# Gate products of the recurrent branch in two row halves of the array, and the fifth and sixth chunk's steps moved to later rounds

## The chip, the cores and the metric

The kernel runs on one core of a Trainium2 chip. The metric is the device time of the whole program in microseconds (us). A core has five engines that run side by side, each through its own instruction list in order: TensorE (PE, matrix products into PSUM), VectorE (DVE), ScalarE (ACT), GpSimd (POOL) and SyncE (SP), which here only issues DMA transfers. They wait for one another through semaphores.

## The reference, cut to what matters

One layer of a streaming encoder runs on 2048 prompt tokens and 64 sample tokens. The change touches one of its two token mixers, the recurrent one (RG-LRU), with 512 channels in eight blocks of 64:

```
xb = x.reshape(B, T, 8, 64)
r  = sigmoid(einsum('btni,nij->btnj', xb, wa) + ba)      # gate a
ig = sigmoid(einsum('btni,nij->btnj', xb, wx) + bx)      # gate x
log_a = -8 * r * softplus(-lam);  a = exp(log_a)
u  = sqrt(-expm1(2 * log_a)) * (ig * x)
h_t = a_t * h_{t-1} + u_t                                 # a scan over the tokens
rnn = h * gelu(rg)
```

`x` is here a causal convolution of width 4 of one projection (`rx`), `rg` is another. The gates are therefore block-diagonal products: channel block n reads only its own 64 channels. The other mixer is attention over a band of 512 past tokens. Both are projected from the same normed input by one wide matrix, `w_in`.

## The kernel before, in words

The program has stages one behind the other: modulation and values (to about 145 us), the projections (145 to 769 us), attention (from 769 us), the merge of the two mixers, the output projection, and the feed-forward part.

The stage in question is the projection stage. It has 16 rounds, four for each j = 0..3; a j is 128 of the 512 recurrent channels. Round i = r % 4 of a j is of kind RECUR (i = 0: `rx` and `rg`), GATES (i = 1 and 3: merge gates) or HEADS (i = 2: queries and keys). A round is seven products c = 0..6 of a fast matrix scheme (sums and differences of quarter matrices, as in Strassen's). Each product has three column pieces q of 352 tokens, and each piece 12 matmuls (four contraction tiles by three passes over f16 high and low parts): 36 matmuls for a product, 252 for a round, all in `passes` at L2988. PE also makes the gate products, six chunks s = 0..5 of 353 tokens for each j (L3029, `gate_products`): six matmuls each, two gates by three passes, into PSUM banks 4 and 5. `GATE_SLOTS` says behind which product of which round they stand.

The other engines run the lists that are written out for each round:

- ACT splits the next weights into their high part (`proj_hi`, L1377), copies products out of PSUM (`copy`, L1398, and `c21`, L1416 to L1419), applies the gate functions (`gates`: L1482 and L1485 read banks 4 and 5 with tanh, L1488 and L1489 make tanh and exp), takes the root (`root`, L1494, which needs another function table than tanh), and makes high parts: of a chunk (`chunk_hi`), of the recurrent output (`rnn_hi`, L1500), of the queries (`q_hi`, L1441) and of the keys (`k_hi`, L1447).
- DVE makes the low parts of all these (`proj_lo` L2159, `rnn_lo` L2307, `q_lo` L2231, `k_lo` L2236), adds products up (`p_block`, L2220 to L2226), makes the convolution (`conv`), and the recurrence (`recur1`, `recur2` with the scan at L2282 or L2287, `rnn_product` L2301).
- SP issues, in this order, in the loop over rounds: the next round's weights, then in i = 1 and i = 2 the stores of the recurrent output, then in i = 3 the stores of queries and keys. Behind the last round it issues the loads of the attention stage.

```
                if i == 2:
                    for s in range(3, NS):
                        recurrent_store(j, s)      # waits x_lo: the low part of chunk s
                if i == 3:
                    head_row(j, 0)                 # waits qk_lo: queries' low part
                    new_keys(j)                    # waits qk_hi: keys' high part
                    head_row(j, 1)                 # waits qk_lo: keys' low part
```

PE may not write product c = 2 before ACT has copied c = 0 of the same piece out of its bank, nor c = 4, 5, 6 before the copies of c = 2, 3, 4; a gate product waits for its chunk's low part (`x_xlo`); and product c = 1 of rounds 1 to 3 waits, as `gates_before` says, until ACT has read the gate products out of bank 4.

## Time and profile before

| | |
|---|---|
| median of three runs | 2694.84 us (2688.36 to 2695.31) |
| span of the profiled execution | 2692.3 us, 2.5 us under that median |
| PE busy | 2645.6 us, 98% of the span |
| DVE, ACT, POOL busy | 65%, 51%, 23% |
| mean granted clock of PE | 0.992 of full speed |
| chain that ended last | PE 84%, DVE 5%, ACT 4%, DMA 3%, issue 2% |

The profiled execution's own time is its span, from the first to the last instruction, and the little that lies around it; the medians of runs take in both. An engine's busy share is a mean over all stages, so what a change in one stage is worth is read in that stage.

### The profile page before, as it was taken

Reading aid. Unit: us, or ns where it says so; the run is one execution under the profiler, and the core shown is the slowest. Engines: PE = TensorE matmul, PEld = TensorE weight load, DVE = VectorE, ACT = ScalarE, POOL = GpSimd, SP = SyncE. Lnnn points to the kernel's source line nnn. Section 1 sums busy time; section 2 is a strip of 40 time slices with the busy share of each in tenths; the row PEclk is TensorE's granted clock in tenths of the full one; section 3 lists DMA queues with packets and bytes.
Section 4 is the critical chain, followed back from the end, with each engine's and each line's share of the span. In section 5 each row is a group of like instructions: output and inputs, shape, how many; then the busy total and the mean of one; then the engine's idle time right before and its main releaser. Section 6 shows DMA issues by size and latency. Waiting matters only on the chain.

```text
span 2692.3 us, 50625 instructions
## 1 busy us (share of the span) xinstructions
PE 2645.6 (98%) x18664; PEld 1771.5 (66%) x18664; DVE 1750.8 (65%) x3367; ACT 1362.9 (51%) x2666; POOL 628.2 (23%) x698
## 2 busy tenths in 40 slices
PE   7999999999999999999999999999999999999998
PEld 2466666666668888557996666666666666666665
DVE  4966464655646666776778788888888875242433
ACT  4967474755656666113556555565555653121211
POOL 2600000000008889000000254433344311101000
PEclk9999999999999999999999999999999999999999
DMA  8621322031294442556552354445545438567572
GB/s 281 200 74 66 135 78 105 25 109 71 93 231 95 112 156 105 183 210 202 143 142 69 126 181 166 171 168 189 181 159 179 165 120 325 212 233 262 210 249 106
DMA packets 238419, 423.07 MB, mean 157 GB/s; under 512 B 57816, under 2 KB 162776, under 8 KB 230056
## 3 DMA queue, kind: packets, MB, share of 16 engines
q1 hardware_dynamic: 229400, 412.03, 46.1%
q10 hardware_dynamic: 8848, 8.74, 1.0%
q8 instruction: 109, 1.79, 0.3%
q14 instruction: 62, 0.51, 0.1%
HBM read 283.42 MB, written 139.92 MB: 157 GB/s over the span
## 4 chain that ended last, share of the span: by engine, by line
PE 84%; DVE 5%; ACT 4%; DMA 3%; issue 2%; POOL 1%; SPq 0%; DVEq 0%; ACTq 0%; POOLq 0%
PE ps L2988 57%; PE ps L3240 14%; PE ps L3080 4%; PE ps L3067 3%; PE ps L3056 2%; DMA arena<-in_w_mod_rest 2%; PE ps L2912 1%; ACT arena L1600 1%; PE ps L3094 1%; POOL arena L1140 1%; PE ps L3029 1%; DVE arena L2393 1%; DVE arena L2471 1%; ACT arena L1607 1%; DVE arena L2089 0%
## 5 line engine op out<-in xcount | busy, mean ns | idle before, releaser
L2988 PE MATMUL ps<-arena 128*128 128x352 f16 (+1 forms) x11880 | 1613.1, 297 | 5.1 <-ACT arena L1768 2.1
L2988 PEld LDWEIGHTS ps<-arena 128*128 128x128 f16 x11880 | 1100.6, 97 | 513.1 <-ACT arena L1768 2.5
L3240 PE MATMUL ps<-arena 128*128 128x352 f16 x2772 | 414.9, 310 | 0.5 <-DVE arena L2689 0.5
L3240 PEld LDWEIGHTS ps<-arena 128*128 128x128 f16 x2772 | 264.7, 96 | 150.8 <-issue 1.0
L1197 POOL TENSOR_TENSOR arena<-arena 128x128 f32<-128x128 f32 x44 | 30.6, 695 | 740.4 <-DMA arena<-in_w_down 740.1
L3094 PE MATMUL ps<-arena 128*128 128x424 f16 (+1 forms) x960 | 172.5, 341 | 2.1 <-DVE arena L2471 1.4
L1760 ACT ACTIVATE arena<-ps 128x352 f32<-128x352 f32 x264 | 116.3, 460 | 98.8 <-PE ps L2988 98.8
L1153 POOL CAST arena<-arena 64x512 f16<-64x512 f32 x8 | 4.9, 610 | 689.6 <-DMA arena<-in_cache_kT 689.3
L3080 PE MATMUL ps<-arena 128*128 128x64 f32 (+2 forms) x1200 | 151.0, 272 | 0.5 <-DVE arena L2435 0.5
L1207 POOL TENSOR_TENSOR arena<-arena 128x176 f32<-128x176 f32 (+1 forms) x57 | 56.2, 986 | 398.4 <-DMA arena<-ffn_hidden 398.4
L3080 PEld LDWEIGHTS ps<-arena 128*128 128x128 f32 (+2 forms) x1200 | 144.4, 193 | 3.4 <-issue 2.1
L3094 PEld LDWEIGHTS ps<-arena 128*128 128x128 f16 x960 | 92.1, 96 | 82.0 <-DVE arena L2471 2.2
L1398 ACT ACTIVATE arena<-ps 128x352 f32<-128x352 f32 x192 | 81.0, 463 | 123.2 <-PE ps L2988 123.2
L2792 DVE TENSOR_TENSOR arena<-ps,arena 128x352 f32<-128x352 f32 x12 | 6.3, 525 | 206.3 <-PE ps L3240 176.4
L2592 DVE SCALAR_TENSOR_TENSOR arena<-arena 128x512 f16<-128x512 f32 x154 | 105.4, 715 | 49.4 <-ACT arena L1722 49.4
L1607 ACT ACTIVATE arena<-ps 128x512 f32<-128x512 f32 (+3 forms) x136 | 76.3, 561 | 104.7 <-PE ps L3067 104.6
L2660 DVE SCALAR_TENSOR_TENSOR arena<-arena 128x2114 f32<-128x2114 f32 x44 | 110.1, 2502 | 27.1 <-ACT arena L1797 27.0
L1181 POOL TENSOR_TENSOR arena<-arena 128x1024 f32<-128x1024 f32 (+6 forms) x147 | 119.7, 814 | 13.6 <-POOL arena L1174 3.7
L2159 DVE SCALAR_TENSOR_TENSOR arena<-arena 128x512 f16<-128x512 f32 x112 | 73.9, 687 | 64.1 <-ACT arena L1377 63.9
L1953 ACT ACTIVATE arena<-ps 128x352 f32<-128x352 f32 x12 | 5.6, 464 | 205.7 <-PE ps L3240 205.7
L2664 DVE SCALAR_TENSOR_TENSOR arena<-arena 128x2114 f32<-128x2114 f32 x44 | 108.8, 2473 | 0.3
L1797 ACT ACTIVATE arena<-arena 128x2114 f32<-128x2114 f32 x44 | 94.5, 2147 | 26.7 <-DVE arena L2647 26.4
(239 smaller groups left out, 3587.1 us busy)
## 6 DMA issues: line engine op xcount, KB each, us to landing
hidden_combinations<-arena SPq DMA_DIRECT2D x48, 616.0 KB, 3.2
arena<-hidden_combinations SPq DMA_DIRECT2D x24, 1232.0 KB, 7.8
arena<-in_w_up SPq DMA_DIRECT2D x44, 512.0 KB, 4.9
down_combinations<-arena SPq DMA_DIRECT2D x44, 448.0 KB, 2.8
ffn_hidden<-arena SPq DMA_DIRECT2D x44, 440.0 KB, 3.1
arena<-down_combinations SPq DMA_DIRECT2D x10, 1792.0 KB, 7.8
arena<-down_combinations SPq DMA_DIRECT2D x20, 896.0 KB, 6.9
arena<-ffn_hidden SPq DMA_DIRECT2D x50, 352.0 KB, 3.9
```

The source lines that it names most:

```text
L1181: pool.tensor_tensor(out, djunk[:, :, 0:w], djunk[:, :, w:2 * w], ALU.add).then_inc(ada_step, 1)
L1398: act.activation(pcp[(0, 1, 2, 0)[i]][q], ps[:, bank, 0:CF], ACT.Copy, scale=CSF).then_inc(p_cp, 1)
L1607: act.activation(pt[:, x.h, 0:m * P], ps[:, 4, 0:m * P], ACT.Copy).then_inc(t_act, 1)
L1760: act.activation(fcp[(0, 1, 2, 0)[i]][q], ps[:, bank_of((0, 2, 3, 4)[i], q), 0:CF], ACT.Copy, scale=CSF)\
L1797: act.activation(out, u[:, 0:LF], ACT.Identity, scale=w0, bias=fb).then_inc(f_tap, 1)
L2592: dve.scalar_tensor_tensor(fsp[:, c, :, 1, :], src.rearrange("p (k m) -> p k m", k=4), -WSF if c == 6 else WSF, fsp[:, c, :, 0, :], ALU.mu ...
L2660: dve.scalar_tensor_tensor(out, u[:, 1:1 + LF], tap(1), out, ALU.mult, ALU.add).then_inc(f_conv, 1)
L2664: dve.scalar_tensor_tensor(out, u[:, 2:2 + LF], tap(2), out, ALU.mult, ALU.add).then_inc(f_conv, 1)
L2988: mm = pe.matmul(out, wt[:, k, wp, :], act_t[:, k, hp], start=(first and k == 0 and n == 0), stop=(last and k == K - 1 and n == 2), skip_g ...
L3080: mm = pe.matmul(ps[0:x.rows, 6, 64 * x.h:64 * x.h + 64], pt[0:k, x.h, c * P:c * P + x.rows], vv[x.b][0:k, x.v0 + c, 64 * x.h:64 * x.h + 6 ...
L3094: mm = pe.matmul(out, wt[:, wp, k, :], mixT[:, k, hp, t:t + w], start=(k == k0 and m == 0), stop=(k == k1 - 1 and m == 2))
L3240: mm = pe.matmul(ps[:, down_bank(n, k), 0:CF].rearrange("p (w t) -> p w t", w=2), dwt(i)[:, wi, wp, :], dact[i][:, :, bi, hp, :], start=(i ...
```

## The change

Two things are done at once.

1. The gate weights were a matrix of 128 by 128 for each gate, zero outside its two blocks. Now the two gates share one matrix of 128 by 128: gate a has its blocks on the diagonal, gate x off it (the input that holds gate x's bias is shifted by 64 rows to match). A gate product is six matmuls again, but each takes only 64 rows of the array: channels 0 to 63 with all 128 weight columns go to bank 4, channels 64 to 127 to bank 5, in turn. Bank 4 then holds gate a for the low channels and gate x for the low channels in its upper half; bank 5 the same for the high channels. ACT reads each half by itself: four tanh of 64 partitions in place of two of 128.
2. The steps of the fifth and sixth chunk (s = 4 and 5), and the root of the fourth, move to later rounds on PE, ACT and DVE. SP's list stays as it was.

```
-            return NS * j + (0, 2, 5, 6)[i]
+            return NS * j + (0, 2, 4, 6)[i]          # gates_before
...
             def gates(j, s):
-                act.wait_ge(x_gate, 2 * n + 1)
+                low, high = slice(0, 64), slice(64, 128)
+                act.wait_ge(x_gate, 2 * n + 2)
                 act.wait_ge(x_conv, 3 * n + 3)
-                act.activation(cols, ps[:, 4, 0:w], ACT.Tanh, scale=0.5 * CS, bias=half_bias(0, j)).then_inc(x_act, 1)
-                act.wait_ge(x_gate, 2 * n + 2)
+                act.activation(cols[low], ps[low, 4, 0:w], ACT.Tanh, scale=0.5 * CS, bias=half_bias(0, j)[low])
+                act.activation(cols[high], ps[high, 5, 0:w], ACT.Tanh, scale=0.5 * CS, bias=half_bias(0, j)[high])\
+                    .then_inc(x_act, 1)
-                act.activation(bufI[s % 2][:, 0:w], ps[:, 5, 0:w], ACT.Tanh, scale=0.5 * CS, bias=half_bias(1, j)).then_inc(x_act, 1)
+                act.activation(bufI[s % 2][low, 0:w], ps[high, 4, 0:w], ACT.Tanh, scale=0.5 * CS,
+                               bias=half_bias(1, j)[high])
+                act.activation(bufI[s % 2][high, 0:w], ps[low, 5, 0:w], ACT.Tanh, scale=0.5 * CS,
+                               bias=half_bias(1, j)[low]).then_inc(x_act, 1)
...
             def gate_products(j, s):
-                r = 4 * j + (0, 0, 1, 1, 1, 2)[s]
+                r = 4 * j + (0, 0, 1, 1, 2, 2)[s]
-                for g in range(2):
-                    for m, (wp, hp) in enumerate(PASSES):
-                        mm = pe.matmul(ps[:, 4 + g, 0:w], gws[:, wp, P * g:P * g + P], xsp[hp][:, 0:w],
+                for m, (wp, hp) in enumerate(PASSES):
+                    for g in range(2):
+                        own = slice(64 * g, 64 * g + 64)
+                        mm = pe.matmul(ps[:, 4 + g, 0:w], gws[own, wp, :], xsp[hp][own, 0:w],
                                        start=(m == 0), stop=(m == 2))
-                    mm.then_inc(x_gate, 1)
+                        if m == 2:
+                            mm.then_inc(x_gate, 1)
...
-            GATE_SLOTS = {(0, 3): 0, (0, 5): 1, (1, 2): 2, (1, 4): 3, (1, 6): 4, (2, 2): 5}
+            GATE_SLOTS = {(0, 3): 0, (0, 5): 1, (1, 2): 2, (1, 4): 3, (2, 2): 4, (2, 4): 5}
```

The rest of the diff moves the calls. On ACT the root of chunk 3 goes from the end of round 1 to the start of round 2, `gates(4)`, `root(4)`, `rnn_hi(4)` and `gates(5)` spread over round 2, and `root(5)`, `q_hi`, `rnn_hi(5)` go into round 3. The largest shift is at the head of the fourth round of each j. On DVE, these are the rows of the end of round 2 and the start of round 3 for the last j, before (L2278 to L2301 is the recurrence of chunk 5, L2307 `rnn_lo`, L2231 `q_lo`, L2236 `k_lo`, L2220 `p_block` of product c = 1):

```order
L2278 TENSOR_TENSOR arena<-arena 128x350
L2287 SCALAR_TENSOR_TENSOR arena<-arena 128x283
L2288 SCALAR_TENSOR_TENSOR arena<-arena 128x64
...
L2307 SCALAR_TENSOR_TENSOR arena<-arena 128x350
L2159 SCALAR_TENSOR_TENSOR arena<-arena 128x4x128
L2223 SCALAR_TENSOR_TENSOR arena<-ps,arena 128x352 x2
L2223 SCALAR_TENSOR_TENSOR arena<-ps,arena 128x320
L2223 SCALAR_TENSOR_TENSOR arena<-ps,arena 128x32
L2231 SCALAR_TENSOR_TENSOR arena<-arena 128x2115
L2159 SCALAR_TENSOR_TENSOR arena<-arena 128x4x128 x2
L2236 TENSOR_TENSOR arena<-arena 128x2115
L2220 SCALAR_TENSOR_TENSOR arena<-ps,arena 128x352 x2
```

The same place on DVE in the changed kernel, whose lines stand five higher (L2283 to L2306 the recurrence, L2236 `q_lo`, L2225 `p_block`, L2241 `k_lo`, L2312 `rnn_lo`):

```order
L2164 SCALAR_TENSOR_TENSOR arena<-arena 128x4x128 x2
L2283 TENSOR_TENSOR arena<-arena 128x350
L2292 SCALAR_TENSOR_TENSOR arena<-arena 128x283
L2293 SCALAR_TENSOR_TENSOR arena<-arena 128x64
...
L2306 TENSOR_TENSOR arena<-arena 128x64
L2236 SCALAR_TENSOR_TENSOR arena<-arena 128x2115
L2225 SCALAR_TENSOR_TENSOR arena<-ps,arena 128x352 x2
L2225 SCALAR_TENSOR_TENSOR arena<-ps,arena 128x320
L2225 SCALAR_TENSOR_TENSOR arena<-ps,arena 128x32
L2241 TENSOR_TENSOR arena<-arena 128x2115
L2312 SCALAR_TENSOR_TENSOR arena<-arena 128x350
```

The recurrence of chunk 5 and `q_lo` have moved behind the two `proj_lo` that open round 3, `k_lo` behind the sums of product c = 1, and `rnn_lo(5)` from the middle of round 2 to behind `k_lo`.

On ACT the head of round 3 for the last j read so before (L1416 to L1419 `c21`, L1377 `proj_hi`, L1447 `k_hi`, L1398 the copies; `q_hi`, L1441, stands at the end of round 2):

```order
L1441 ACTIVATE arena<-arena 128x2115
L1416 ACTIVATE arena<-ps 128x352 x2
L1418 ACTIVATE arena<-ps 128x320
L1419 ACTIVATE arena<-ps 128x32
L1377 ACTIVATE arena<-arena 128x4x128 x2
L1447 ACTIVATE arena<-arena 128x2115
L1398 ACTIVATE arena<-ps 128x352 x12
```

And so in the changed kernel (L1499 `root`, L1505 `rnn_hi`):

```order
L1377 ACTIVATE arena<-arena 128x4x128 x2
L1499 ACT_TABLE_LOAD
L1499 ACTIVATE arena<-arena 128x350
L1441 ACTIVATE arena<-arena 128x2115
L1398 ACTIVATE arena<-ps 128x352 x3
L1447 ACTIVATE arena<-arena 128x2115
L1505 ACTIVATE arena<-arena 128x350
L1398 ACTIVATE arena<-ps 128x352 x9
```

The table load, the root and `q_hi` now stand ahead of the copies of c = 0, and `k_hi` and `rnn_hi(5)` behind them.

SP's list for the same place is word for word that of before (L734 to L737 stores of the recurrent output, L722 and L723 of queries and of keys, L775 and L778 the first loads of the attention stage); the waits of each row stand in brackets:

```order
L734 DMA recurrent_outputs<-arena 256x1x353 [waits x_lo] x2
L736 DMA recurrent_outputs<-arena 256x1x283 [waits x_lo]
L737 DMA recurrent_outputs<-arena 256x1x64
L722 DMA queries<-arena 256x1x2048 [waits qk_lo]
L723 DMA queries<-arena 256x1x64
L727 DMA out_k_prompt<-arena 128x512 [waits qk_hi]
...
L722 DMA keys<-arena 256x1x2048 [waits qk_lo]
L723 DMA keys<-arena 256x1x64
L775 DMA arena<-queries 64x2112 [waits k_stored,q_stored,p_filled]
```

What has moved is only when `x_lo` of chunk 5 and the two `qk_lo` come, on which these rows wait.

## Rows read from the trace of the kernel before

**Rows 1.** The page: busy time by engine.

```profile
PE 2645.6 (98%) x18664; PEld 1771.5 (66%) x18664; DVE 1750.8 (65%) x3367; ACT 1362.9 (51%) x2666; POOL 628.2 (23%) x698
```

**Rows 2.** Stretches: the second and fourth round of j = 1, and round 15.

```profile
340.80:381.10 40.30, 40.30 (x272) 26.07 (x271) 28.39 (x56) 32.03 (x53) 0.00 (x0) 1.00 0.12 41
419.50:457.20 37.70, 37.70 (x255) 24.40 (x253) 14.29 (x24) 15.53 (x27) 0.00 (x0) 1.00 0.27 94
731.00:768.50 37.50, 37.50 (x254) 24.22 (x251) 8.88 (x17) 12.94 (x22) 0.00 (x0) 1.00 0.89 232
```

The columns are the stretch, its length, busy us (and instructions) of PE, PEld, DVE, ACT and POOL, the granted clock, the DMA share and GB/s.

**Rows 3.** Timeline of PE around a gate product: start, us, instruction.

```profile
167.09 1.06 PE L3029 MATMUL ps<-arena 128*128 128x353 f16 x6
167.99 10.90 PE L2988 MATMUL ps<-arena 128*128 128x352 f16 x72
```

**Rows 4.** Timeline of PE: full-height, then half-height matmuls between those of L2957.

```profile
115.61 1.02 PE L2957 MATMUL ps<-arena 128*128 128x512 f16 x4
116.47 0.60 PE L2927 MATMUL ps<-arena 128*128 128x128 f32 x4
...
126.74 0.81 PE L2957 MATMUL ps<-arena 128*128 128x512 f16 x3
127.48 0.43 PE L2927 MATMUL ps<-arena 64*128 64x64 f32 x2
127.84 0.39 PE L2957 MATMUL ps<-arena 128*128 128x512 f16 x1
...
840.33 0.40 PE L3067 MATMUL ps<-arena 64*128 64x64 f32 x4
```

**Rows 5.** Groups of ACT in round 2 of j = 1.

```profile
L1398 ACT ACTIVATE arena<-ps 128x352 f32<-128x352 f32 x12 | 4.9, 467 | 1.9 <-PE ps L2988 1.9
L1494 ACT ACT_TABLE_LOAD x2 | 2.6, 1283 | 0.0
L1482 ACT ACTIVATE arena<-ps,arena 128x350 f32<-128x350 f32 x1 | 0.6, 554 | 0.0
```

**Rows 6.** Timelines of ACT and DVE: round 2 of j = 1, then round 15.

```profile
406.99 0.81 DVE L2287 TENSOR_TENSOR_SCAN arena<-arena 128x283 f32<-128x283 f32 x1
410.91 0.52 DVE L2307 SCALAR_TENSOR_TENSOR arena<-arena 128x350 f16<-128x350 f32 x1
...
731.63 1.15 ACT L1377 ACTIVATE arena<-arena 128x512 f16<-128x512 f32 x2
732.67 1.97 ACT L1447 ACTIVATE arena<-arena 128x2115 f16<-128x2115 f32 x1
734.67 2.36 DVE L2236 TENSOR_TENSOR arena<-arena 128x2115 f16<-128x2115 f32 x1 [1.08 <-ACT arena L1447]
741.96 0.59 DVE L2220 SCALAR_TENSOR_TENSOR arena<-ps,arena 128x320 f32<-128x320 f32 x2 [1.26 <-PE ps L2988]
```

**Rows 7.** Timeline of SP's queue in round 15.

```profile
730.86 0.51 SPq L722 DMA_DIRECT2D queries<-arena  x1
735.05 1.63 SPq L728 DMA_DIRECT2D out_k_sample<-arena  x1
741.95 1.16 SPq L775 DMA_DIRECT2D arena<-queries  x2
763.03 0.59 SPq L787 DMA_DIRECT2D arena<-in_cache_v  x1
```

**Rows 8.** DMA busy tenths, 731 to 769 us, in 40 slices.

```profile
DMA  0999351499501999999999999999998999999996
```

**Rows 9.** Landing of L787, and PE where attention begins.

```profile
DMA to landing us min/median/max: 4.7/5.0/5.4
...
772.07 0.34 PE L3080 MATMUL ps<-arena 128*128 128x64 f32 x2
```

**Rows 10.** Stretches around a pause of PE.

```profile
1500.00:1508.00 8.00, 5.89 (x41) 3.61 (x39) 5.01 (x11) 4.12 (x8) 1.88 (x4) 1.00 0.31 100
1508.00:1511.40 3.40, 3.40 (x13) 1.70 (x12) 3.40 (x4) 3.40 (x5) 2.09 (x2) 0.50 0.20 73
```

72 lines of the change are left out of this document (36 added, 36 removed).

## The prediction

> **What bounds the kernel now.** I read the page first: PE is busy 98% of the span [rows 1], so where PE never waits, only less PE time or a new wait of PE can move the end. Then the stretches: in the second and the fourth round of j = 1 and in round 15, PE is busy for exactly the length of the stretch, at full granted clock, while ACT has 32.03 of 40.30 us in round 1 and 15.53 of 37.70 us in round 3 [rows 2]. The reader is to see that this stage is PE alone: ACT and DVE are only of interest where they come so late that PE would stop, and the work moved from round 1 to rounds 2 and 3 moves from a full list to an empty one without gaining anything by itself. Last I read the place where the stage hands over to attention: there the DMA engines are at 9 tenths or more in nearly all slices from 743 us on [rows 8]. Nothing waits for them yet, but with little to spare, as worked out below.
>
> **Term 1, the gate products.** The six matmuls of L3029 start at 167.09 us and the next L2988 at 167.99 us: 0.90 us, or 0.15 us for each [rows 3]. There are 24 such groups, 21.6 us in all. The changed group has as many matmuls of as many columns, but in three pairs whose two members use different rows of the array and different banks. If the members run side by side, three pairs take 3 x 0.15 = 0.45 us; if not, 0.90 us as before. No row shows two half-height matmuls in different halves, so both stay in the range. I take side by side, because two matmuls on separate rows share neither weights nor outputs, and give the other a chance of its own below. The Trainium skill says the same ("TensorE: Matmul & The Clock Gate", measured speedup vs the span model: tiles of one packing start about 4 ns apart). By that rule a pair would be an estimated 0.154 us, and the group 0.46 us; no run here shows it yet.
>
> What speaks against it is the border between full and half height. Four L2957 matmuls before a full-height L2927 start at 115.61 us, 0.215 us apart by their width and clock, and L2927 starts at 116.47 us, just 4 x 0.215 us later: no delay. Before the half-height L2927, three start at 126.74 us, so the last at 127.17 us, and L2927 starts at 127.48 us: 0.31 us behind it, 0.09 us more than its streaming. A matmul's time has a tail behind its streaming: a single L2957 takes 0.39 us, 0.18 us over its 0.215 us. Four half-height ones in a row take 0.40 us, less that tail 0.07 us apiece. The two of L2927 should then need 0.14 us until the next can start, but that starts at 127.84 us, 0.36 us behind the first: 0.22 us more. Half of it, 0.11 us, lies between the two (0.43 us in all, less 0.25 us for the second, less 0.07 us), and is theirs as f32 with a weight load of their own, as I read it; the other half is the way out [rows 4]. I take the way in and the way out, 0.09 + 0.11 = 0.20 us a group, and keep 0 and the whole 0.31 us as bounds. The changed group is then 0.45 + 0.20 = 0.65 us, which saves 0.25 us, times 24 = **6.0 us**. Bounds: 0.14 x 24 = 3.4 us and 0.45 x 24 = 10.8 us. The Trainium skill has a rule for this border ("TensorEngine Tiling (Array Packing)", key properties: a change of tiling mode drains TensorE, a change of tile does not); the 0.09 us ahead of the half-height L2927 agrees with it [rows 4]. By its reading every group pays twice, as the sum has it.
>
> **Term 2, ACT and DVE within the rounds: nothing.** Four tanh of 64 partitions replace two of 128. A tanh on 353 columns takes 0.55 us [rows 5]; columns set its length, so two more cost 1.1 us a chunk, two chunks in a round, 2.2 us. If halves took half the time it would be nothing. Round 1 has 8 us of ACT free [rows 2], loses `root(3)` with the table loads that it brought (1.28 us each [rows 5]) and the fifth chunk. Where could PE stop? Time is counted from a round's start, and a product is 36 x 0.149 = 5.4 us, so c = 2 starts at 10.7 us and needs the first copy of c = 0 by then.
> - Round 2: ACT's first part is as before until about 3.2 us, then root(3) (1.28 + 0.5), `rnn_hi(3)` behind the scan and the product on DVE (2.3 us) and its own 0.5 us: 7.8 us. The first copy takes 0.47 us [rows 5], ready at 8.3 us: 2.4 us to spare. Later, gates(4) with its table load ends near 21.5 us and root(4) near 24.6 us; the copies of c = 3 are done by 25.8 us and wanted from 27.4 us on: 1.6 us or more to spare.
> - Round 3: `proj_hi` starts 0.6 us into the round and takes 1.05 us [rows 6], root(5) ends at 3.5 us, DVE's recurrence of chunk 5 at 5.4 us (its scan is 0.81 us [rows 6]), `q_hi` as long as `k_hi`, 1.97 us, at 7.4 us. First copy at 7.9 us: 2.8 us to spare.
> If the cover of 1.6 us were gone, each us beyond would cost 4 us, once for every j. What is late next is only what waits for the low parts: the queue.
>
> **Term 3, the handover to attention: 5.5 us lost.** SP's list is in order. The stores of queries and keys, and behind them the first loads of attention, stand behind the store of chunk 5, which waits for `rnn_lo(5)`. That used to be done in round 2: at 410.91 us for j = 1 [rows 6], 8.6 us before round 3. Now it stands behind `k_lo` in round 3. For the last j, counted from 731.0 us:
> - `q_hi` 7.4, `q_lo` as long as `k_lo`, 2.36 us: 9.8. `p_block` of c = 1 can't end before PE has made it: as now, 741.96 + 0.59 us [rows 6], so 11.5. `k_hi` behind three copies: 8.5 + 1.97 = 10.5, no wait. `k_lo` 11.5 + 2.36 = 13.9. `rnn_lo(5)` 0.52: 14.4.
> - SP: two stores of chunk 5 in 1.2 us (each issue as the 0.51 us of L722, and the rest between), queries 1.2, new keys 2.0 (L728 alone 1.63), keys 1.2 [rows 7]: 20.0 us. The load of L775 is issued there. Now it is issued at 741.95 us, 10.95 us in [rows 7]. It is 9.05 us late.
> - By the DMA engines' time it is more. Now the stores of queries and keys lie in two bursts in the first 12 slices, whose tenths add up to 64, so 6.1 us and, since a 9 is 90% or more, up to 6.9 us: 6.5 us. The loads fill every slice from the 14th on, 12.4 us in, and the first burst begins 1.1 us behind its issue [rows 7, 8]. Then the stores' transfer begins at 15.6 + 1.1 = 16.7 us in one piece, ends at 23.2 us, and the loads' behind it: 10.8 us late.
> The last of the values (L787) is issued at 763.03 us and lands 4.7 us later, 767.7 us [rows 7, 9]. PE wants it for the first L3080 at 772.07 us [rows 9]: 4.4 us to spare. So PE stops for 9.05 - 4.4 = 4.7 us by SP's time, or 10.8 - 4.4 = 6.4 us by the DMA engines'. I take the middle, 5.5 us. PE's own end moves with round 15, so nothing of term 1 gives cover here. For j = 0 to 2 the same lateness hits the weights for the next round 0, due by the end of round 3, 20 us later: nothing.
>
> **Term 4, the clock.** At 1500 us PE is busy 5.89 of 8.00 us, and the next 3.40 us run at a granted clock of 0.50, the 1.2 GHz level, with PE busy throughout [rows 10]: half of that, 1.7 us, was lost. A stop of some 5 us at the handover should bring such a stretch. Attention's first units leave PE partly idle anyhow, so I take 1.0 us, between 0 and 1.7 us.
>
> **Sum.** -6.0 + 0 + 5.5 + 1.0 = +0.5 us. On the profiled span of 2692.3 us that is 2692.8 us; on the median, 2.5 us higher, **2695.3 us**. Its own range: -8.6 (borders cost 0.09 us) + 4.7 + 0 = -3.9 us, to -3.4 + 6.4 + 1.7 = +4.7 us: 2691 to 2700 us.
>
> **The rivals.**
> - *The handover costs nothing.* DVE, ACT or the stores are faster than I chained them, or the loads don't need the time they take now, so that the 4.4 us hold. For it: a slice or two ahead of the loads are empty today [rows 8], and the stores might move beside the loads. Against it: a lateness of 9 us is twice the reserve. It gives -6.0 us, 2688.8 us; with free borders -10.8 us, 2684 us. Only below a group of 0.56 us does this end faster than can be told. Chance 0.20.
> - *The halves don't run side by side* (the change doesn't do what it says, slower). Then a group is 0.90 + 0.20 us: +4.8 us in place of -6.0 us, and with the handover 4.8 + 6.5 = +11.3 us, 2706.1 us. It decides from a pair of 0.26 us on, where 24 x 3 pairs x 0.11 us have made the time 8.1 us longer than my sum. For it: no row shows two halves at once. Against it: they share nothing. Chance 0.15.
> - *Copies come late in rounds 2 or 3.* ACT now waits there for a scan on DVE ahead of the copies of c = 0. If the chain is 2 us longer than its spare, PE stops 2 us in each j: 0.5 + 8 = +8.5 us, 2703.3 us. Against it: 1.6 to 2.8 us to spare by durations that overlap by 0.1 us each. Chance 0.05.
>
> **How the numbers follow.** Mine 0.60, the rivals 0.20, 0.15, 0.05. About 0.3%, 8.1 us, is what a measurement of this kernel can tell from no change: below 2686.8 us it is faster, above 2702.9 us slower. Faster: 0.07 of the free handover, 0.03 of mine, 0.10. Slower: 0.13 of the halves, 0.03 of the copies, 0.01 of mine, 0.17. The same: 0.73. The range 2687 to 2706 us leaves out some 0.10 below and 0.09 above.
>
> **What would show it.** The start of L2988 behind a gate group, minus the group's start: 0.65 us if right, 1.1 us if the halves take turns. PE's idle time in 145 to 763 us: none. SP's first L775: 20 us behind the start of round 15. PE's idle time at the first L3056, L3067 and L3080, put down to DMA, band, values or queries: 5 to 7.5 us, and a granted clock of 0.50 behind it. The prediction is wrong if PE doesn't wait there, or if the group isn't between 0.45 and 0.76 us.

## The result and the profile after

| | before | changed |
|---|---|---|
| median of five runs each | 2695.14 us | 2738.13 us (2730.72 to 2740.86) |
| span of the profiled execution | 2692.3 us | 2736.3 us |
| ratio, 95% interval | | 1.0156 (1.0141 to 1.0171): slower by 42 us |

The prediction was 2695.3 us, 2687 to 2706 us. The time lies 32 us above the top of the range.

The page of the changed kernel, busy time by engine (against [rows 1]):

```profile
PE 2649.0 (97%) x18664; PEld 1763.3 (64%) x18664; DVE 1751.6 (64%) x3367; ACT 1393.0 (51%) x2714; POOL 628.9 (23%) x698
```

PE has 3.4 us more busy time, and the span is 44 us longer: PE waits more. So the first question is where. I cut both spans at PE's own instructions: the projection stage runs from the first start to the last start of a product matmul of 352 columns, the handover from there to the first start of L3080 (L3087 in the changed kernel).

| us | before | changed | difference |
|---|---|---|---|
| ahead of the projection stage | 145.6 | 144.8 | -0.8 |
| projection stage | 622.9 | 659.7 | +36.9 |
| handover to attention | 3.6 | 11.1 | +7.5 |
| attention, merge and the rest | 1920.2 | 1920.7 | +0.5 |

**The part that was right.** Timeline of PE around a gate product (the place of [rows 3]):

```profile
166.37 0.62 PE L3035 MATMUL ps<-arena 64*128 64x353 f16 x6
166.92 10.91 PE L2993 MATMUL ps<-arena 128*128 128x352 f16 x72
```

The next product starts 0.55 us behind the group's start; before it was 0.90 us. The rest of the cost stands ahead of the group: its first matmul starts 0.245 us behind the last full-height one, where two full-height ones are 0.149 us apart. The whole group then costs 0.651 us, for which the prediction had 0.65 us. In single records the two members of a pair start 4 ns apart.

**Where PE stops.** Waits of PE in the changed kernel (what it waited for, us in total, times, longest). Before, PE had no wait in the projection stage at all:

```profile
PE ps L3035 <- DVE arena L2225: 26.6, 4, 7.4
PE ps L2993 <- ACT arena L1416: 5.6, 5, 1.2
PE ps L3063 <- DMA arena<-keys: 5.1, 1, 5.1
PE ps L2993 <- ACT arena L1419: 1.0, 4, 0.2
PE ps L3087 <- DMA arena<-in_cache_v: 1.4, 1, 1.4
```

The first row is the answer: once for every j, PE waits 6.4 to 7.4 us at one gate group. It is the group of chunk 4, which the change moved behind product c = 2 of round 2. Timeline of PE in round 2 of j = 1 (the round starts at 388.97 us):

```profile
388.97 3.74 PE L2993 MATMUL ps<-arena 128*128 128x352 f16 x24 [1.24 <-ACT arena L1416]
392.95 12.81 PE L2993 MATMUL ps<-arena 128*128 128x352 f16 x84 [0.24 <-ACT arena L1419]
412.12 1.07 PE L3035 MATMUL ps<-arena 64*128 64x353 f16 x6 [6.36 <-DVE arena L2225]
413.12 13.37 PE L2993 MATMUL ps<-arena 128*128 128x352 f16 x72
```

The 72 matmuls behind the stop take 13.37 us, where 72 others took 10.91 us. The stretches show why (length, busy of PE, PEld, DVE, ACT, POOL, granted clock, DMA share, GB/s):

```profile
406.80:412.10 5.30, 0.00 (x0) 0.01 (x1) 1.69 (x7) 0.00 (x0) 0.00 (x0) 0.60 1.01 412
412.10:418.10 6.00, 5.98 (x24) 2.82 (x25) 4.74 (x9) 4.23 (x7) 0.00 (x0) 0.50 0.09 24
```

While PE stands, the granted clock falls to 0.50, the 1.2 GHz level, and here it stays there for the first 6 us of full work; at the other three places for 2.8 to 3.3 us. At the four places together, the matmuls behind the groups take 5.2 us more than at full clock, and four small waits of 0.11 us at product c = 2 make it 5.7 us.

**What the stop waits for.** The gate products go to banks 4 and 5, where product c = 1 of the same round stands until DVE has read it. So PE waits for the sums L2225 of product c = 1, and DVE had long been idle. DVE in the same round:

```profile
396.84 0.53 DVE L2283 TENSOR_TENSOR arena<-arena 128x353 f32<-128x353 f32 x1 [6.44 <-ACT arena L1499]
397.40 0.95 DVE L2287 TENSOR_TENSOR_SCAN arena<-arena 128x353 f32<-128x353 f32 x1
398.68 0.53 DVE L2306 TENSOR_TENSOR arena<-arena 128x353 f32<-128x353 f32 x1
399.77 0.53 DVE L2312 SCALAR_TENSOR_TENSOR arena<-arena 128x353 f16<-128x353 f32 x1 [0.57 <-ACT arena L1505]
400.22 1.29 DVE L2164 SCALAR_TENSOR_TENSOR arena<-arena 128x512 f16<-128x512 f32 x2
410.41 1.45 DVE L2225 SCALAR_TENSOR_TENSOR arena<-ps,arena 128x352 f32<-128x352 f32 x4 [8.91 <-DMA gates<-arena]
```

DVE waits 8.91 us for a store: L2225 writes into the row buffer from which SP still stores the gate row of round 1. SP's queue, changed kernel:

```profile
401.53 0.81 SPq L690 DMA_DIRECT2D arena<-in_w_proj  x2
402.38 0.43 SPq L716 DMA_DIRECT2D gates<-arena  x1
403.89 0.99 SPq L717 DMA_DIRECT2D gates<-arena  x1
```

And before:

```profile
384.40 0.80 SPq L690 DMA_DIRECT2D arena<-in_w_proj  x2
385.25 0.43 SPq L716 DMA_DIRECT2D gates<-arena  x1
```

SP's list is in order. The store of the gate row (L716, L717) stands behind the load of the next weights (L690), which waits until DVE has made the low parts of this round's last two weight tiles (L2164). Before, these were made 3.4 us into the round. Now they stand behind `recur2`, the product and `rnn_lo` of chunk 3, and these behind the moved root(3) (L1499): L2164 ends 12.5 us into the round, and L690 is issued at once. The whole chain, read backwards: PE's gate group, DVE's sums, the stores, SP's weight load, DVE's low parts, DVE's recurrence of chunk 3, ACT's root(3). Each link is one row above. The wait itself is not new: before, the group of chunk 5 stood behind c = 2 of round 2 and waited for the same sums. That round starts at 381.04 us:

```profile
393.19 1.45 DVE L2220 SCALAR_TENSOR_TENSOR arena<-ps,arena 128x352 f32<-128x352 f32 x4
397.15 1.05 PE L3029 MATMUL ps<-arena 128*128 128x350 f16 x6
```

There the sums began 12.2 us into the round, now 21.4 us, and the group, 16.1 us in, did not stop. So what costs the time is the late store, and not that another chunk's group now stands in that place.

Adding up PE's start-to-start times over the whole stage gives its parts, in us over what 4031 matmuls of 352 columns take at 0.1487 us each:

| | before | changed |
|---|---|---|
| 24 gate groups | 21.6 | 44.3 = 24 x 0.65 + 28.7 |
| half clock behind them, with the four small waits | 0 | 5.7 |
| stops at copies (L1416, L1419) | 0 | 8.0 |
| all small rest | 1.9 | 2.3 |

The 28.7 us are what the four groups of chunk 4 take (7.5 to 8.5 us each) beyond 0.65 us. The differences, 22.7 + 5.7 + 8.0 + 0.4, are the stage's +36.9 us.

**The handover.** SP, PE and DVE in the changed kernel around the last round, which starts at 767.05 us (against [rows 7, 9]):

```profile
778.50 2.35 DVE L2241 TENSOR_TENSOR arena<-arena 128x2115 f16<-128x2115 f32 x1
780.77 0.52 DVE L2312 SCALAR_TENSOR_TENSOR arena<-arena 128x350 f16<-128x350 f32 x1
...
787.65 2.15 SPq L775 DMA_DIRECT2D arena<-queries  x2
...
809.88 0.59 PE L3063 MATMUL ps<-arena 128*128 128x128 f16 x4 [5.06 <-DMA arena<-keys]
812.01 0.60 PE L3063 MATMUL ps<-arena 128*128 128x256 f16 x2 [1.55 <-DVE arena L2419]
815.64 0.69 PE L3087 MATMUL ps<-arena 128*128 128x64 f32 x2 [1.40 <-DMA arena<-in_cache_v]
```

`k_lo` (L2241) ends 13.8 us and `rnn_lo(5)` (L2312) 14.2 us into the round; the prediction had 13.9 and 14.4. L775 is issued 20.6 us into it; the prediction had 20.0. So the chain of term 3 on DVE and SP happened nearly as written. On PE's side it did not quite: the prediction let PE stop for the values (L787) at the first L3080, but the largest part, 5.06 us, was a wait for the keys at the first L3063, and 1.40 us one for the values.

### The profile page after: what moved, and what is told of

The parts are those of the page before. It is cut to its first block, busy times and chain, and to the rows that moved or that the text cites. A ratio compares the mean times of both kernels' runs of the same rounds, so it can differ in the third digit from the quotient of the medians.

```text
span 2736.3 us, 50651 instructions
## 1 busy us (share of the span) xinstructions
PE 2649.0 (97%) x18664; PEld 1763.3 (64%) x18664; DVE 1751.6 (64%) x3367; ACT 1393.0 (51%) x2714; POOL 628.9 (23%) x698
## 4 chain that ended last, share of the span: by engine, by line
PE 77%; ACT 7%; DVE 6%; DMA 3%; issue 3%; POOL 1%; SPq 1%; DVEq 0%; ACTq 0%; POOLq 0%
PE ps L2993 47%; PE ps L3247 15%; PE ps L3101 5%; PE ps L3087 4%; PE ps L3074 3%; PE ps L3063 2%; DMA gates<-arena 1%; PE ps L2917 1%; ACT arena L1605 1%; DMA arena<-in_w_down 1%; POOL arena L1140 1%; DVE arena L2253 1%; ACT arena L1315 1%; ACT arena L1281 1%; ACT arena L1612 1%
## 5 line engine op out<-in xcount | busy, mean ns | idle before, releaser
L2993 PE MATMUL ps<-arena 128*128 128x352 f16 (+1 forms) x11880 | 1619.2, 298 | 12.6 <-ACT arena L1416 5.6
L2993 PEld LDWEIGHTS ps<-arena 128*128 128x128 f16 x11880 | 1099.4, 97 | 531.2 <-issue 11.1
L3087 PE MATMUL ps<-arena 128*128 128x64 f32 (+2 forms) x1200 | 151.0, 271 | 1.9 <-DMA arena<-in_cache_v 1.4
L3087 PEld LDWEIGHTS ps<-arena 128*128 128x128 f32 (+2 forms) x1200 | 144.6, 192 | 4.6 <-DMA arena<-in_cache_v 1.7
L2597 DVE SCALAR_TENSOR_TENSOR arena<-arena 128x512 f16<-128x512 f32 x154 | 105.0, 713 | 46.1 <-ACT arena L1727 46.1
L1398 ACT ACTIVATE arena<-ps 128x352 f32<-128x352 f32 x192 | 79.4, 458 | 93.1 <-PE ps L2993 93.1
L1808 ACT ACTIVATE arena<-arena 128x1057 f32<-128x1057 f32 x44 | 45.3, 1076 | 124.9 <-DVE arena L2669 124.9
L1605 ACT ACTIVATE arena<-arena 128x640 f32<-128x640 f32 (+5 forms) x136 | 102.8, 756 | 10.0 <-DVE arena L2419 9.8
```

The costliest lines, as they stand in the source:

```text
L1605: act.activation(pr[0:x.rows, x.h, 0:x.w], pr[0:x.rows, x.h, 0:x.w], ACT.Exp, scale=-1.0, bias=least[0:x.rows, x.h:x.h + 1], accum_out=sm[ ...
L2597: dve.scalar_tensor_tensor(fsp[:, c, :, 1, :], src.rearrange("p (k m) -> p k m", k=4), -WSF if c == 6 else WSF, fsp[:, c, :, 0, :], ALU.mu ...
L2993: mm = pe.matmul(out, wt[:, k, wp, :], act_t[:, k, hp], start=(first and k == 0 and n == 0), stop=(last and k == K - 1 and n == 2), skip_g ...
L3087: mm = pe.matmul(ps[0:x.rows, 6, 64 * x.h:64 * x.h + 64], pt[0:k, x.h, c * P:c * P + x.rows], vv[x.b][0:k, x.v0 + c, 64 * x.h:64 * x.h + 6 ...
```

## The experiments

Fourteen kernels. All ratios are against the kernel before, in runs on the same chip; stage and handover are cut as in the table above. Before has 622.87 and 3.61 us, the changed kernel 659.72 and 11.14 us.

| run | stage | handover | median (before beside it) | ratio, 95% interval |
|---|---|---|---|---|
| e1 gate stores first | 625.75 | 10.95 | 2705.00 (2694.24) | 1.0040 (1.0027 to 1.0054) |
| e2 halves only | 630.13 | 3.61 | 2701.90 (2694.24) | 1.0027 (1.0012 to 1.0043) |
| e3 moves only | 652.75 | 10.44 | 2729.13 (2694.24) | 1.0137 (1.0102 to 1.0172) |
| e4 split low parts first | 626.25 | 10.89 | 2704.50 (2694.24) | 1.0042 (1.0026 to 1.0057) |
| e5 head rows first | 625.76 | 5.56 | 2699.59 (2694.01) | 1.0016 (1.0005 to 1.0028) |
| e6 first copy first | 623.80 | 6.22 | 2697.71 (2694.01) | 1.0014 (1.0003 to 1.0025) |
| e7 halves in turn | 625.90 | 10.61 | 2705.02 (2694.01) | 1.0037 (1.0024 to 1.0050) |
| e8 moves, stores first | 622.88 | 10.59 | 2700.86 (2694.01) | 1.0027 (1.0017 to 1.0037) |
| e9 whole copy first | 622.18 | 5.98 | 2696.02 (2695.21) | 1.0008 (0.9997 to 1.0019) |
| e10 loads first | 622.19 | 3.72 | 2697.67 (2695.21) | 1.0012 (1.0000 to 1.0024) |
| e11 all in time | 618.08 | 3.61 | 2693.15 (2692.98) | 0.9998 (0.9986 to 1.0010) |
| e12 as e11, full height | 622.88 | 3.61 | 2700.31 (2692.98) | 1.0020 (1.0008 to 1.0032) |
| e13 last rows first | 618.09 | 3.61 | 2691.47 (2692.80) | 0.9988 (0.9977 to 1.0000) |
| e14 as e13, full height | 622.88 | 3.61 | 2697.57 (2692.80) | 1.0011 (1.0000 to 1.0023) |

**e1, the stores ahead of the weights.** The theory is the chain above; the rival is that the low parts or the recurrence themselves are too late for PE. Only SP's list changes:

```
                 j, i = r // 4, r % 4
+                if i == 2:
+                    gate_row(r - 1, 0)
+                    gate_row(r - 1, 1)
                 if r + 1 < NR:
                     round_tiles(r + 1)
...
-                if r and kind_of(r - 1) == GATES:
+                if r and i == 0:
                     gate_row(r - 1, 0)
```

> The changed kernel, but in round 2 of each j SP issues the stores of the merge gates' rows ahead of the next round's weights, not behind them. Theory (queue): the 6.4 to 7.4 us for which PE stops at the fifth chunk's gate products are the landing of these stores, on which DVE's sums of product c = 1 wait; they are late only because the weights ahead of them wait for the low parts of products 5 and 6, now behind the fourth chunk's recurrence. Then the wait of 26.6 us and most of the half-clock stretch behind it go: 2738 - 27 - 7 = 2704 us, between 2700 and 2709 us. Rival (load): DVE and ACT are late by themselves in round 2 and the store only ends last by a little; then another releaser takes its place, and no more than a third goes: above 2725 us. Rival (half height): the products in halves cost the time; then nothing changes, 2738 us.

Measured: 2705.0 us. SP in the same round, and what is left of the waits in the stage:

```profile
382.86 0.33 SPq L716 DMA_DIRECT2D gates<-arena  x1
385.73 0.46 SPq L717 DMA_DIRECT2D gates<-arena  x1
391.88 0.81 SPq L690 DMA_DIRECT2D arena<-in_w_proj  x2
...
PE ps L2996 <- ACT arena L1419: 5.6, 5, 1.2
PE ps L2996 <- ACT arena L1422: 1.0, 4, 0.2
```

The weights are as late in the round as in the changed kernel (12.6 us into it, since this one starts at 379.3 us), and PE doesn't mind. The wait at the gate group is gone in all four j, the stage is 34.0 us shorter. One line's place in SP's list was 31 us of the 42 us by the ratios.

**e4, the other link of the chain.** In place of SP's order, DVE makes the low parts ahead of the recurrence of chunk 3:

```
+                if i == 2:                    # behind proj_lo of products 5 and 6
+                    recur2(j, 3)
+                    rnn_product(j, 3)
+                    rnn_lo(j, 3)
...
-                if i == 1:                    # ahead of them
-                    recur2(j, 3)
-                    rnn_product(j, 3)
-                    rnn_lo(j, 3)
```

> The changed kernel, but on DVE the low parts of products 5 and 6 stand ahead of the fourth chunk's recurrence at the start of round 2. SP's list is not touched. Theory (queue): the weights and behind them the gate rows' stores are issued some 6 us earlier (about 3 to 4 us into the round, as before the change), land near 12 us, and PE's 6.4 us stop shrinks to under 1 us: 2700 to 2710 us. Rival (load): the recurrence itself makes DVE late, and it is still there: above 2725 us. If only e1 helps, it is the weights' transfer ahead of the stores and not the recurrence.

Measured: 2704.5 us, stage 626.25 us. Cutting the chain at either link gives the same, within 0.5 us of the stage: it is one chain.

**e2 and e3, each half of the change alone.** e2 keeps every step at its place of before and has the products in halves. e3 has the moved steps and the full-height products. In both, `gate_products` names the round of chunk 4 to match its slot.

```
e2: with the changed gates() and gate_products(), but
             GATE_SLOTS = {(0, 3): 0, (0, 5): 1, (1, 2): 2, (1, 4): 3, (1, 6): 4, (2, 2): 5}
e3: with the gates() and gate_products() of before, but
             GATE_SLOTS = {(0, 3): 0, (0, 5): 1, (1, 2): 2, (1, 4): 3, (2, 2): 4, (2, 4): 5}
```

> The kernel before with the gate products in two row halves and the four half tanh, but every step of chunks 4 and 5 where it was. Theory (queue): the group costs 0.65 us in place of 0.90 us, so -6 us, and ACT in round 1 gets three chunks of two more tanh (3.3 us) against about 2 us that its copy of the next round's first product has to spare, so PE stops 1 to 4 us in each j: -6 + (4 to 16) = 2693 to 2705 us. The handover to attention stays as before. Rival (half height): the products themselves cost the time, and this kernel is near 2738 us.

> The kernel before with the moved steps of the fourth to sixth chunk alone; the gate products have full height and ACT reads them with two tanh. Theory (queue): all of the loss is in the moves: PE stops in round 2 of each j for the stores as in the changed kernel, and at the handover to attention, so 2738 + 6 us for the full-height groups, less up to 6 us since ACT ends round 1 earlier: 2738 to 2744 us. Rival (half height): near 2695 us. Rival (load, ACT): without the longer tanh ACT is in time, and the wait is much shorter: 2710 us or less.

Measured: e3 2729.13 us, e2 2701.90 us. The moved steps alone bring the stop, of 4.9 us at most and 19.5 us in all, so shorter than with halves (26.6 us); e3 is 9 us faster than the least that I had expected. But the halves alone are slower than before as well, by 7.3 us of stage, although each group costs 0.65 us. ACT and PE in e2, end of round 1 of j = 1:

```profile
379.23 0.50 ACT L1475 ACTIVATE arena<-arena 128x353 f16<-128x353 f32 x1
...
380.39 0.63 PE L3035 MATMUL ps<-arena 64*128 64x353 f16 x6 [1.41 <-issue]
381.65 17.95 PE L2993 MATMUL ps<-arena 128*128 128x352 f16 x108 [0.63 <-ACT arena L1416]
```

The group of chunk 4, with the wait at the copy behind it, costs 2.8 us there, in every j. It needs `chunk_hi(4)` (L1475) and DVE's low part (0.53 us) behind it, and L1475 ends at 379.73 us: as I read it, the two more tanh of each of its chunks (0.55 us apiece) made it late, since the full-height kernel of before has no stop there. Added up as above, e2's groups take 10.2 us beyond 24 x 0.65 us (four of 2.8 us, and three of chunk 5 of 1.2 us), the half clock behind them 1.6 us, one copy 0.8 us and the rest 0.6 us more: 13.2 - 5.9 = 7.3 us. So with halves ACT's list of round 1 is too long as it stands. Whether another order in it would have done as well as moving work out, no run tells: none has halves, nothing moved and another order. My view of [rows 2], 8 us of ACT free in round 1, did not show that: the free time lies elsewhere in the round than at its end.

**e8, the moves with the stores first.** The edit of e1 on e3:

> e3 (moves alone, full-height products) with the gate rows' stores ahead of the weights in round 2. Theory (queue): e3's 19.5 us of waits and the half clock behind them go, and the 7 us of the handover stay: 2695 + 7 = 2702 us, 2699 to 2705 us. Against e1 it tells what the halves are worth by themselves: -6 us of the groups and about +7 us of the late copy, so no difference. Rival (load): the recurrence moved into rounds 2 and 3 makes DVE late itself: above 2712 us.

Measured: stage 622.88 us, before's to 0.01 us, and handover 10.59 us, 7.0 us above before's. The run is 7.3 us slower (ratio 1.0027; 6.9 us by the medians). With the stores in place the moved steps cost nothing in the stage, and all that they lose is the handover. Between e8 and e1 the stage with halves is 2.9 us longer, though the groups save 5.9 us: the stops at copies (the rows under e1) take 8.0 us and smaller waits 0.8 us, and e8 has none of them. So these stops belong to the halves and not to the moved steps.

**e7, the halves one behind the other.** e1 with the loops exchanged, so that a half's three passes stand together:

```
-                for m, (wp, hp) in enumerate(PASSES):
-                    for g in range(2):
+                for g in range(2):
+                    for m, (wp, hp) in enumerate(PASSES):
```

> e1, but the three passes of one half stand ahead of the three of the other, so that only the third of the one and the first of the other can lie side by side. Theory (side by side): a group then takes 5 times 0.15 us and the borders' 0.20 us, 0.95 us in place of 0.65 us, times 24 = 7 us more than e1: 2712 us. Rival (the saving is only that half-height matmuls are cheap): as e1, 2705 us.

Measured: 2705.02 us, and my expectation was wrong. Timeline of PE:

```profile
165.53 0.63 PE L3038 MATMUL ps<-arena 64*128 64x353 f16 x6
166.10 10.91 PE L2996 MATMUL ps<-arena 128*128 128x352 f16 x72
```

The group takes 0.57 us from its start to the next product, as in pairs. Six in turn would take 0.90 us. The list has three matmuls of rows 0 to 63 and then three of rows 64 to 127; in the single records the starts are still in pairs, 10 ns apart instead of 4. So this run says nothing on what pairs are worth (e12 and e14 do), but, if the instructions reach PE in the order of the kernel's text, that PE ran a matmul of the one half past two of the other. The trace records neither that order nor which half a matmul is on, so this is my reading of the starts. The Trainium skill says the contrary of the reading ("TensorE: Matmul & The Clock Gate", part 3 on packing small matmuls: matmuls start and end strictly in program order). The group's length here does not agree. That the rival (half-height matmuls that are merely cheap, one behind the other) is wrong, the same starts tell: two lie 4 or 10 ns apart, and the next two follow 0.15 to 0.16 us later.

**e5, the order of the last stores.** e1, and SP stores chunk 5 behind the queries, the new keys and the keys:

```
                 if i == 2:
-                    for s in range(3, NS):
+                    for s in range(3, NS - 1):
                         recurrent_store(j, s)
                 if i == 3:
                     head_row(j, 0)
                     new_keys(j)
                     head_row(j, 1)
+                    recurrent_store(j, NS - 1)
```

> e1 and in SP's list the sixth chunk's store behind the stores of queries and keys, not ahead of them. Theory (queue): at the handover to attention PE stops from its last product to the first L3080 for 10.95 us in e1 against 3.61 us before, since the loads of keys, bias and values start some 9 us late behind that store. Ahead of it they start about 4 us late, and the stores before them are spread: 4 to 5.5 us to the first L3080, so 5 to 7 us less, with the half-clock stretch there shorter by some: 2697 to 2700 us. Rival (the loads are slow for another reason, as the DMA engines being full): no more than 2 us less.

Measured: handover 5.56 us against 10.95 us, 2699.59 us. So the store of chunk 5 ahead of the heads' stores is shown to be the cause of 5.4 of the 7.3 us that e1's handover has over that of before; most of the rest goes with e10.

**e6 and e9, copies ahead of high parts.** e6 is e5 with ACT's first two copies of round 1's last product ahead of `chunk_hi(4)`, and with DVE's low part of chunk 4 behind the sums of c = 5 of round 1. e9 is e6 with the third copy there too, taken from the start of round 2:

```
e6: -                if i == 1:
    -                    chunk_hi(j, 4)
                     if i == 1:
                         c21(r, 0)
                         c21(r, 1)
    +                    chunk_hi(j, 4)
    ...
    +                for q in range(3):
    +                    p_block(r, 1, q)
                     if i == 1:
                         chunk_lo(j, 4)
    -                for q in range(3):
    -                    p_block(r, 1, q)
e9: +                    c21(r, 2)
```

> e5 and, at the end of round 1, ACT copies the first two pieces of the last product ahead of the fifth chunk's high part, and DVE makes that chunk's low part behind its sums of c = 5. Theory (queue): PE stops 1.2 and 0.2 us in each j for that copy because it stands behind a chunk whose convolution comes late; these 6.6 us and the tails with them go, and what is left of the change is the groups' 6 us: about 7 us under e5, 2689 to 2693 us, at or under the kernel before. Rival (load): ACT's list of round 1 is too long with the tanh in halves, and the copy stays late: under 2 us less than e5.

> e6 with the third piece's copy too ahead of the merge gates' tanh at the end of round 1. In e6 PE still stops 1.3 us in each j, for this piece: it stands behind a tanh that waits for DVE's sums of c = 5. Theory (queue order): these four stops go, with the small ones behind them, 5 to 6 us less than e6 in the projection stage, which then takes 618 us: 2691 to 2694 us. Rival (the list of ACT is too long in round 1 with halves): the stop moves to a later copy in round 2 and the stage stays above 622 us, 2697 us.

Measured: stages of 623.80 and 622.18 us, medians of 2697.71 and 2696.02 us, both above what I had expected. PE's longest waits in the stage, first in e6, then in e9:

```profile
PE ps L2996 <- ACT arena L1423: 4.6, 4, 1.2
```

```profile
PE ps L2997 <- ACT arena L1402: 3.4, 4, 0.9
```

Each edit removed the stop that it was made for, and the next one in ACT's list appeared, smaller: the third piece's copy, then the copy of c = 0 in round 2 behind `rnn_hi(3)`. In the prediction that last one had 2.4 us to spare.

**e10, the attention's loads first.** e9, and in the last round SP issues the loads of attention ahead of the keys' store and chunk 5's:

```
                     new_keys(j)
+                    if r + 1 < NR:
                         head_row(j, 1)
                         recurrent_store(j, NS - 1)
...
             values_and_bias(0)
+            head_row(NJ - 1, 1)
+            recurrent_store(NJ - 1, NS - 1)
```

> e9, and in the last round the loads of the attention stage ahead of the stores of keys and of the sixth chunk. Theory (queue): what is left of the handover, from the last product to the first L3080 (6.2 us in e6, 3.6 us before the change), is the transfer of those two stores ahead of the loads; it falls to 3.6 to 4.5 us. With e9's gain the kernel is then the groups' 6 us faster than before the change, less what is left in the rounds: 2688 to 2691 us. Rival: the loads are late because of the stores of queries and new keys, or for the DMA engines being full anyway; then as e9.

Measured: handover 3.72 us, nearly as before (3.61 us), and still no gain (2697.67 us where I had expected 2688 to 2691 us). What it gave, PE lost again 13 us later at one exp (longest wait 3.2 us; below).

**e11 and e12, all in time, with halves and without.** e10, and ACT copies c = 0 of round 2 ahead of `rnn_hi(3)`; root(3) stays ahead of the copies, other than the text on record says. e12 is the same with full-height products.

```
                 if i == 2:
                     root(j, 3)
-                    rnn_hi(j, 3)
...
                 for q in range(3):
                     copy(r, 0, q)
+                if i == 2:
+                    rnn_hi(j, 3)
```

> The last repaired version (gate rows stored ahead of the weights, the copies of chunk 4 and the third piece ahead of the high parts, the attention's loads ahead of the last stores), and now also the copy of c = 0 in round 2 ahead of root(3) and rnn_hi(3) on ScalarE. Theory (nothing is left but the order of copies on ScalarE): the 3.4 us of stops at that copy go, the projection stage takes 617 to 618 us (622.87 of before less 24 x 0.25), the time is 2690 to 2694 us, 1 to 5 us under before. Rival (ScalarE has too much work in rounds 1 and 2 for any order, since a tanh of 64 partitions costs as much as one of 128): the stop only moves to another copy or product, the stage stays above 621 us and the time within 2 us of the version before it (2697.7).

> The same moved steps and the same order of stores, copies and loads, but the gate products over the full height of the array, as before: this run against the last one is what the halves alone are worth. Theory (the halves give back 0.25 us at each of 24 gate groups): the projection stage takes about 622.9 us, and the time is 5 to 6 us above that of the version with halves. Rival (what the halves save is lost in waits that follow): both take the same time within 2 us.

Measured: 2693.15 and 2700.31 us. PE has no stop left in the stage but one of 0.8 us, in round 1 of j = 0. The stage is 618.08 us with halves and 622.88 us without: **4.8 us is what the halves are worth there** (6.0 us of the groups, less the stop and small waits), and the medians are 7.2 us apart, for which I had expected 5 to 6 us. Yet against before the ratio is 0.9998 (0.9986 to 1.0010): the 4.8 us don't arrive. The trace of e11 shows one more place, ACT and PE in attention:

```profile
777.34 0.63 ACT L1684 ACTIVATE arena<-arena 128x512 f32<-128x512 f32 x1 [2.65 <-issue]
...
779.21 0.66 PE L3082 MATMUL ps<-arena 128*128 128x128 f32 x4 [2.65 <-ACT arena L1613]
```

L1684 writes where the last gate rows and the recurrent output lie, and waits for their stores. SP issues the last of them behind a wait for the keys' store, which e10 had made late.

**e13 and e14, the last gate rows first.** e11 and e12, and in SP's list behind the last round:

```
             sp.wait_ge(p_filled, p_done(NR - 1, 6, 2))
+            gate_row(NR - 1, 0)
+            gate_row(NR - 1, 1)
             sp.wait_ge(q_stored, 32 * NJ)
             sp.wait_ge(k_stored, 32 * NJ)
             later_tile(0)
             cached_keys(0)
-            gate_row(NR - 1, 0)
-            gate_row(NR - 1, 1)
```

> The last repaired version with halves, and in SP's list behind the last round the stores of the last gate rows now stand ahead of the wait for the stores of queries and keys. Theory (ScalarE's L1684 waits for the gate rows' stores, which SP issues at 769.9 to 772.4 us, 6 us behind the last product, because it waits for the keys' store first): the rows are issued some 4 us earlier, the waits of 2.65 us on ScalarE and of 2.65 us on PE behind it go, the first attention units run at full clock, and the time is 2.5 to 5 us under that of the version before it, 2688 to 2691 us, and under before by 2 to 5 us. Rival (the gain goes elsewhere, by clock or by other waits of attention): the wait goes and the time stays within 1.5 us of 2693.2 us.

> The same with gate products over the full height. Theory: the 3.9 us wait at the same place goes, the projection stage stays at 622.9 us as before, so that the time is that of before within 1.5 us, and 4 to 6 us above that of the run with halves beside it. Rival: it stays at 2700 us, so the 5 us that this version lost against before lie elsewhere.

Measured: 2691.47 and 2697.57 us. The last of the gate rows' stores in e11, and then that store and ACT's L1684 in e13:

```profile
770.77 1.61 SPq L717 DMA_DIRECT2D gates<-arena  x1
```

```profile
767.62 0.79 SPq L717 DMA_DIRECT2D gates<-arena  x1
...
775.29 0.63 ACT L1684 ACTIVATE arena<-arena 128x512 f32<-128x512 f32 x1
```

The store is issued 3.2 us earlier and the wait is gone. The ratio is 0.9988 (0.9977 to 1.0000): 3.2 us under before by the ratio, 1.3 us by the medians, and since the interval reaches 1.0000, "faster" is not shown. I had expected 2 to 5 us and a median of 2688 to 2691 us, so the size stays undecided between theory and rival. e14 was to be within 1.5 us of before and is 4.8 us above it: missed. Halves against full height are 6.1 us apart, for the second time more than the stage's 4.8 us.

Where the gain of e13 went in its profiled execution can be read in attention. Attention, from the handover to the first matmul of 424 columns, in before, e11 and e13:

```profile
772.07:1071.41 299.34, 291.75 (x2338) 243.30 (x2337) 187.11 (x850) 191.10 (x475) 234.12 (x214) 0.97 0.46 132
```

```profile
766.60:1067.79 301.19, 291.73 (x2339) 243.82 (x2338) 187.17 (x850) 191.10 (x475) 234.01 (x214) 0.97 0.48 137
```

```profile
766.24:1071.81 305.57, 296.76 (x2338) 248.04 (x2338) 189.00 (x850) 190.93 (x475) 239.79 (x216) 0.94 0.47 135
```

The instructions are the same; the granted clock is not, 0.97 and 0.94. The part of it at 0.50 is 20.5 us before, 21.1 us in e11 and 35.4 us in e13, and half of 14.9 us more is 7.5 us, about the 6.2 us by which e13's attention is longer; one new wait of PE, 2.35 us at 1046.88 us, is in it too. Attention leaves PE partly idle in all of them, 291.75 of 299.34 us busy before. In the profiled execution of e13 these stretches ate its gain; its runs go from 2685.1 to 2695.1 us, those of before beside it from 2686.8 to 2700.7 us. What decides how many of them come in an execution, and whether the moved steps bring more of them on the mean, no run here tells. In e14 it is another place: its attention takes 299.80 us, as before, and 3.6 us more lie behind it, from the first matmul of 424 columns to the next one of `passes` (178.99 against 175.43 us). PE's waits there are 1.6 us longer; what else it is, and why, stays open.

## Why the prediction was wrong

- **Term 1, the halves: right.** 0.651 us a group for 0.65, and 24 x 0.25 = 6.0 us. The rule of the Trainium skill that a change of tiling mode drains TensorE ("TensorEngine Tiling (Array Packing)", key properties) agrees with the rows: 0.10 us more on the way in and 0.09 us on the way out of each group, for which I had 0.09 and 0.11. The sum fits better than its two parts, so a little of the agreement is luck.
- **Term 3, the handover: the late stores and loads right, size a little short.** Predicted 5.5 us and 1.0 us of clock; measured 7.5 us with the clock in it. The times of its chain were off by 0.1 to 0.6 us. It had PE stop for the values alone, and most of the stop was for the keys. (The tenths of the 12 slices add up to 63, not 64, which is 0.1 us.)
- **Term 2, "ACT and DVE within the rounds: nothing", failed, and with it the prediction.** It cost 42.8 us where it had 0 (36.9 us of stage, and the 5.9 us that the halves saved in it). The failing sentence is its last one, "what is late next is only what waits for the low parts: the queue". It names the right thing and then follows only two of the queue's entries, the next weights and chunk 5's store. Between them in SP's list stood the stores of the gate rows, which I had left out of the front part's list of what SP issues. They were issued 9.2 us late, counted from the round's start (13.4 us into it in place of 4.2 us, behind weights at 12.6 in place of 3.4 us), DVE's sums of c = 1 wait for them to land, and PE's gate group behind c = 2 waits for the sums: 28.7 us of stops and 5.7 us of clock and small waits behind them. e1 and e4 show it from two sides.
- **Term 2's spare times were wrong as well.** I let root(3) begin 3.2 us into round 2; it began at 395.01 us, 6.0 us into it. The copies from round 1 and the gate rows' tanh stand ahead of it. `rnn_hi(3)` ended 10.8 us in, not 7.8 us, so the first copy of c = 0 was done 11.1 us in (400.11 us), where PE wants it at 10.7 us; that cost only 0.11 us in each j. The larger stops were at the round's border, at the copies of round 1's last product. They stand behind `chunk_hi(4)`, which waits for the convolution on DVE. It stood ahead of them before the change as well, and in e8, with full-height products, PE doesn't stop there; with four tanh to a chunk it does. The stops at these copies took 8.0 us. The rival "copies late" had 8 us too and a chance of 0.05, but for other copies, those of c = 0 in rounds 2 and 3: that the sizes agree is chance.
- **The sum by the runs.** Halves -5.9, stops at chunk 4's groups +28.7, clock and small waits behind them +5.7, stops at copies +8.0, small rest +0.4: the stage's +36.9 us. Handover +7.5, all other stages -0.3: +44.1 us, the spans' difference within 0.1 us.
- **Rivals.** Halves that don't pair (0.15): ruled out by the group's length. Free handover (0.20): ruled out. None had a transfer that PE waits for within the stage.

## What to carry over

When a step is moved past an in-order queue, write down all entries of that queue between the moved release and the end of the round, and for each the buffer it frees and who writes that buffer next. A late store is as good as a late engine: here 9 us on a store that nobody seemed to read became a stop of PE by way of a buffer. Free time of an engine summed over a round says nothing about the end of the round, and when a stop is removed, ask for the next entry of the same list before counting the gain: behind what e6, e9 and e10 removed, the next wait came to light each time, and that behind e10 (3.2 us) was longer than the one behind e9 (0.9 us).

## What the hardware showed that I had not expected

- Two row halves of the array run side by side even when the list has three matmuls of the one ahead of three of the other: 0.57 us for six of 353 columns, where six of full height take 0.90 us (e7 and [rows 3]). The order is that of the kernel's text, which the trace does not record.
- A tanh on 64 partitions takes 0.55 us, as one on 128 [rows 5]. Halving the height on PE doubled the number of these tanh, and e2 shows the price: 13.2 us of waits and clock in the stage against 5.9 us that the groups save.
- PE at rest for 6 to 7 us brought a granted clock of 0.50 that lasted 2.8 to 6.0 us into its next work, once for every j, and in attention time at that level differed between executions by 14.9 us.
